# Hybrid decoder layer, float32: both MLP products as seven block products instead of eight, with the inner activations stored in HBM between them

## The reference, cut to what matters

```python
h = h + mix @ w_out                            # (520, 2048) @ (2048, 2048)
u = _rmsnorm(h, g_ffn)
h = h + jnp.square(jax.nn.relu(u @ w_up)) @ w_down   # w_up (2048, 8192), w_down (8192, 2048)
e = _rmsnorm(p_l @ w_ple, w_ple_norm) * jax.nn.sigmoid(h @ w_ple_gate)
y = _rmsnorm(h + e, g_final)
```

## Time and profile before

| | |
|---|---|
| median of 3 runs | 2850.12 us (2849.66 to 2850.43) |
| span of the profiled execution | 2847.1 us |
| output projection ends, MLP begins | about 1136 us into the span |
| MLP ends | about 2606 us |
| PE, DVE, ACT, POOL busy over the span | 95%, 46%, 27%, 20% |

### The profile page before, as it was taken

How to read it: one execution, slowest core, us unless ns; L and a number is a source line. 1 busy time by engine, 2 the same in 40 slices (tenths; PEclk the granted TensorE clock), 3 DMA queues, 4 the chain that set the end, 5 groups by cost and what they waited for, 6 DMA issues and landing times.

```text
span 2847.1 us, 50247 instructions
## 1 busy us (share of the span) xinstructions
PE 2696.2 (95%) x21759; PEld 2573.3 (90%) x21759; DVE 1320.5 (46%) x1501; ACT 774.8 (27%) x967; POOL 582.7 (20%) x290
## 2 busy tenths in 40 slices
PE   7999999967767999999999999999999999999998
PEld 7999999923346999999999999999999999999998
DVE  4277877628468224333333433333333333346433
ACT  3111111137643223222222222222222222223222
POOL 0098999300036011100000000000000000002322
PEclk9999999988876999999999999999999999999999
DMA  4388888489813222332333233333333333322233
GB/s 132 107 277 269 279 299 285 138 344 353 311 55 121 86 76 81 104 100 94 97 103 98 90 104 97 98 96 104 102 99 97 96 98 98 103 90 89 90 97 112
DMA packets 294896, 396.43 MB, mean 139 GB/s; under 512 B 14773, under 2 KB 256051, under 8 KB 292982
## 3 DMA queue, kind: packets, MB, share of 16 engines
q1 hardware_dynamic: 271688, 380.23, 40.4%
q10 hardware_dynamic: 22990, 13.01, 1.6%
HBM read 377.71 MB, written 15.58 MB: 138 GB/s over the span
## 4 chain that ended last, share of the span: by engine, by line
PE 79%; DVE 6%; POOL 5%; DMA 4%; issue 2%; SPq 2%; ACT 2%; ACTq 0%; DVEq 0%; POOLq 0%
PE ps L1180 25%; PE ps L1182 25%; PE ps L1185 25%; POOL kpage L1029 4%; DMA kpage<-in_cache_k 2%; DMA vpage<-in_cache_v 2%; DVE wl L1672 1%; PE ps L1280 1%; PE ps L1560 1%; SPq L470 1%; POOL dl L1074 1%; DMA xs<-in_x_sample 0%; ACT wh L608 0%; DVE se L1829 0%; POOL bx L1082 0%
## 5 line engine op out<-in xcount | busy, mean ns | idle before, releaser
L1180 PE MATMUL ps<-uh,wh 128*128 128x260 f32 x4512 | 1184.9, 284 | 20.1 <-DVE wl L1672 14.1
L1182 PE MATMUL ps<-ul,wh 128*128 128x260 f32 x4512 | 1180.5, 283 | 0.0
L1672 DVE TENSOR_TENSOR wl<-raw,wh 128x1024 fp32r<-128x1024 f32 (+1 forms) x418 | 590.4, 1413 | 1242.9 <-ACT wh L608 1242.8
L608 ACT ACTIVATE wh<-raw 128x1024 fp32r<-128x1024 f32 (+1 forms) x418 | 440.6, 1055 | 1803.6 <-PE ps L1185 1755.3
L1185 PE MATMUL ps<-uh,wl 128*128 128x260 f32 x4512 | 907.6, 283 | 0.0
L1180 PEld LDWEIGHTS ps<-uh,wh 128*128 128x128 f32 x4512 | 853.1, 189 | 22.9 <-DVE wl L1672 11.8
L1182 PEld LDWEIGHTS ps<-ul,wh 128*128 128x128 f32 x4512 | 851.3, 189 | 0.0
L1185 PEld LDWEIGHTS ps<-uh,wl 128*128 128x128 f32 x4512 | 696.4, 189 | 0.0
L1180 PE MATMUL ps<-hh,wh 128*128 128x260 f32 x2048 | 536.1, 283 | 0.0
L1182 PE MATMUL ps<-hl,wh 128*128 128x260 f32 x2048 | 534.1, 282 | 0.0
L1185 PE MATMUL ps<-hh,wl 128*128 128x260 f32 x2048 | 410.7, 282 | 0.0
(11 more groups left out here) (340 smaller groups left out, 1502.6 us busy)
## 6 DMA issues: line engine op xcount, KB each, us to landing
kpage<-in_cache_k SPq DMA_DIRECT2D x128, 512.0 KB, 4.9
vpage<-in_cache_v SPq DMA_DIRECT2D x128, 512.0 KB, 6.1
raw<-in_w_up SPq DMA_DIRECT2D x128, 512.0 KB, 3.6
raw<-in_w_down SPq DMA_DIRECT2D x128, 512.0 KB, 3.4
raw<-in_w_in SPq DMA_DIRECT2D x88, 512.0 KB, 4.6
raw<-in_w_out SPq DMA_DIRECT2D x32, 512.0 KB, 3.5
raw<-in_w_ple_gate SPq DMA_DIRECT2D x32, 512.0 KB, 3.4
xt<-in_x_prompt SPq DMA_DIRECT2D x8, 1024.0 KB, 9.0
```

What stands on the lines that cost most here:

```text
L608: A(wh[:, c % 2, 0:elems], raw[:, c % 2, 0:elems], ACT.Copy).then_inc(hi_ready, 1)
L1180: mm(ps[:, bank + 2 * m + f, 0:HALF], h_, xh[:, f * HALF:(f + 1) * HALF], start=st, stop=False)
L1182: mm(ps[:, bank + 2 * m + f, 0:HALF], h_, xl[:, f * HALF:(f + 1) * HALF], start=False, stop=False)
L1672: tt(wl[:, c % 2, 0:elems], raw[:, c % 2, 0:elems], wh[:, c % 2, 0:elems].bitcast(F32), ALU.subtract).then_inc(lo_ready, 1)
```

## The change

**Seven products.** A group of 256 weight columns is seen as 2 x 2 blocks: rows in even and odd tiles of 128, columns in two tiles of 128. The activations are seen as 2 x 2 blocks too: even and odd feature tiles, and two token halves. The 2 x 2 block product is made with seven block products of sums of blocks (Winograd's form) in place of eight. Products accumulate on PSUM banks (`BK`, `OPENS`): a bank's earlier product is read out by ACT or DVE, and a later product is then added on top of it.

**Units.** The work item is now a *unit*: 4 row tiles x 1 column tile x 1 token half x 3 = 12 matmuls, with 128 x 512 weight elements. ACT makes the high part (`unit_hi`), DVE the low part (`unit_lo`), in a ring of four. `w_up` takes 32 groups of 14 units, `w_down` 64 steps of 7 units: 896 units, 10,752 matmuls.

**Sums of weights.** Four of the seven products need sums of weight blocks. POOL makes them: `weight_sum`, 4 per group of `w_up`, 1024 elements each; `down_sum`, 4 per step of `w_down`, 512 elements each.

**Sums of activations.** For `w_up`, POOL makes them once (`operand_sum`), ACT and DVE split all seven operands into high and low parts. For `w_down`, each group of `w_up` gives 256 hidden features: ACT copies products out of PSUM, DVE adds (`hidden_add`, two of 520 elements) and applies relu and scale (`hidden_relu`, 1040 elements), ACT squares, POOL makes three sums (`hidden_sums`: 520, 260, 260 elements), ACT and DVE split (`hidden_hi`, `hidden_lo`).

**Through HBM.** The split hidden operands (7 x 520 numbers a partition, 1.86 MB a group) are stored to `hid_scr`, and come back in 8 parts of 7 loads (1.06 MB a load). All of `w_up` comes before all of `w_down`. The residual `h` goes through HBM too, since its place holds the operands of `w_up`. Each step of `w_down` adds its PSUM results to `hT` in six operations (`down_add`: four of 260 elements, two of 520).

**The weight rows** of `w_up` now come as 1 MB (two DMAs of 512 KB) into three buffers; `rows_used` lets buffer `m` go when its last `unit_lo` and its last `weight_sum` are done. The state updates move from the whole MLP to the `w_down` half. Many semaphores are shared in place of own ones. The core of the diff, blank lines left out:

```diff
-CHUNKS = D_FF // 512
+UPS = D_FF // 256
+PARTS = 8
+DOWNS = PARTS * (D_MODEL // 256)
+X_UP = 14 * UPS
+X_ALL = X_UP + 7 * DOWNS
...
+        hid_scr = nc.dram_tensor("hid_scr", (PARTS, 7, P, 4, T), F32, kind="Internal").ap()
...
+        BK = (3, 1, 0, 3, 2, 1, 3)
+        OPENS = (0, 1, 2, 4)
...
+            def rows_used(m):
+                g = m // 2
+                sp.wait_ge(q_lo, 14 * g + (10 if m % 2 else 2))
+                sp.wait_ge(s_sum, 4 * g + (3 if m % 2 else 4))
...
+            def store_hidden(g):
+                sp.wait_ge(o_hi, O_ALL + 4 * (g + 1))
+                sp.wait_ge(o_lo, O_ALL + 4 * (g + 1))
+                sp.dma_start(hid_scr[g // 4, :, :, g % 4, :].rearrange("i p x -> p i x"),
+                             hst.bitcast(F32).rearrange("p i s x -> p i (s x)")).then_inc(h_st, 16)
...
+            for g in range(UPS):
+                for m in (2 * g + 3, 2 * g + 4):
+                    if m < 2 * UPS and m >= 3:
+                        rows_used(m - 3)
+                        for hf in range(2):
+                            load_rows(m, hf)
+                if 1 <= g < UPS - 1:
+                    store_hidden(g - 1)
...
+            def unit_hi(x):
+                if x < X_UP:
+                    g, i = x // 14, x % 14 // 2
+                    if i in (0, 2, 4):
+                        m = 2 * g + (1 if i else 0)
+                        act.wait_ge(r_in[m % 3], 32 * (m // 3 + 1))
+                    else:
+                        act.wait_ge(s_sum, 4 * g + (1, 3, 5, 6).index(i) + 1)
+                else:
+                    n, i = (x - X_UP) // 7, (x - X_UP) % 7
+                    if i in (0, 2, 4):
+                        act.wait_ge(r_in[n % 2], down_landed(n) + 32)
+                    else:
+                        act.wait_ge(s_sum, 4 * UPS + 4 * n + (1, 3, 5, 6).index(i) + 1)
+                if x < 4:
+                    act.wait_ge(w_used, SL_PLE + x // 2 + 1)
+                else:
+                    act.wait_ge(q_used, x - 3)
...
+            def hidden_hi(g, k):
+                if k == 0:
+                    if g:
+                        act.wait_ge(h_st, 16 * 8 + 16 * g)
+                    act.wait_ge(x_q, g + 1)
+                    A(hst[:, 0:3:2, 0, :], tm[:, :, 0:HALF], ACT.Copy).then_inc(o_hi, 1)
+                    A(hst[:, 5, 0, :], tm[:, 1, HALF:T], ACT.Copy).then_inc(o_hi, 1)
+                elif k == 1:
+                    act.wait_ge(t_h, 3 * g + 2)
+                    A(hst[:, 1:4:2, 0, :], tb[:, 0:2], ACT.Copy).then_inc(o_hi, 1)
+                else:
+                    act.wait_ge(t_h, 3 * g + 3)
+                    A(hst[:, 4:7:2, 0, :], tb[:, 2:4], ACT.Copy).then_inc(o_hi, 1)
...
+            def weight_sum(g, k):
+                r1, r2 = rbuf[2 * g % 3], rbuf[(2 * g + 1) % 3]
+                a11, a21, a12, a22 = r1[:, :, 0:P], r1[:, :, P:2 * P], r2[:, :, 0:P], r2[:, :, P:2 * P]
+                n = 4 * g + k
+                if k == 0:
+                    for m in (2 * g, 2 * g + 1):
+                        pool.wait_ge(r_in[m % 3], 32 * (m // 3 + 1))
+                if n >= 3:
+                    pool.wait_ge(q_lo, 14 * g + (-6, -2, 0, 4)[k])
+                if k:
+                    pool.wait_ge(s_sum, n)
+                out = sring[n % 3]
+                s1, s2 = sring[4 * g % 3], sring[(4 * g + 1) % 3]
+                in0, in1 = ((a21, a22), (s1, a11), (a12, s2), (a11, a21))[k]
+                pool.tensor_tensor(out, in0, in1, ALU.subtract if k else ALU.add).then_inc(s_sum, 1)
...
+            def down_sum(n, k):
+                w = wbuf[n % 2]
+                a11, a21, a12, a22 = w[:, 0, :, 0:P], w[:, 0, :, P:2 * P], w[:, 1, :, 0:P], w[:, 1, :, P:2 * P]
+                if k == 0:
+                    pool.wait_ge(r_in[n % 2], down_landed(n) + 32)
+                if n == 0:
+                    pool.wait_ge(q_lo, X_UP - (2, 2, 0, 0)[k])
+                else:
+                    pool.wait_ge(q_lo, X_UP + 7 * (n - 1) + (2, 4, 6, 7)[k])
+                if k:
+                    pool.wait_ge(s_sum, 4 * UPS + 4 * n + k)
+                in0, in1 = ((a21, a22), (dring[0], a11), (a12, dring[1]), (a11, a21))[k]
+                pool.tensor_tensor(dring[k], in0, in1, ALU.subtract if k else ALU.add).then_inc(s_sum, 1)
...
+            def hidden_sums(g):
+                pool.wait_ge(x_q, g + 1)
+                if g:
+                    pool.wait_ge(o_hi, O_ALL + 4 * g)
+                    pool.wait_ge(o_lo, O_ALL + 4 * g)
+                pool.tensor_tensor(tb[:, 0:4:3], tm[:, :, HALF:T], halves(tm[:, 0]), ALU.subtract).then_inc(t_h, 1)
+                pool.wait_ge(t_h, 3 * g + 1)
+                pool.tensor_tensor(tb[:, 1], tm[:, 1, HALF:T], tb[:, 0], ALU.subtract).then_inc(t_h, 1)
+                pool.wait_ge(t_h, 3 * g + 2)
+                pool.tensor_tensor(tb[:, 2], tm[:, 1, 0:HALF], tb[:, 1], ALU.subtract).then_inc(t_h, 1)
...
+            for g in range(UPS):
+                if g + 1 < UPS:
+                    weight_sum(g + 1, 0)
+                if g:
+                    hidden_sums(g - 1)
+                if g + 1 < UPS:
+                    for k in range(1, 4):
+                        weight_sum(g + 1, k)
+            for n in range(DOWNS):
+                for k in range(4):
+                    down_sum(n, k)
+                if n == 0:
+                    hidden_sums(UPS - 1)
+                if n % 8 == 4:
+                    state_update(n // 8)
...
+            def unit(x, bank, opens, pairs, first, last):
+                pe.wait_ge(q_lo, x + 1)
+                out = ps[:, bank, 0:HALF]
+                for k in range(4):
+                    h_, l_ = whq[:, x % 4, k, :], wlq[:, x % 4, k, :]
+                    mm(out, h_, pairs[:, k, 0, :], start=(opens and first and k == 0), stop=False,
+                       skip_group_check=True)
+                    mm(out, h_, pairs[:, k, 1, :], start=False, stop=False, skip_group_check=True)
+                    z = mm(out, l_, pairs[:, k, 0, :], start=False, stop=(last and k == 3), skip_group_check=True)
+                z.then_inc(q_used, 1)
...
+            def unit_lo(x):
+                dve.wait_ge(q_hi, x + 1)
+                tt(wlq[:, x % 4], unit_weights(x), whq[:, x % 4].bitcast(F32), ALU.subtract).then_inc(q_lo, 1)
...
+            def hidden_lo(g, k):
+                src, at_ = ((tm[:, :, 0:HALF], slice(0, 3, 2)), (tb[:, 0:2], slice(1, 4, 2)),
+                            (tb[:, 2:4], slice(4, 7, 2)))[k]
+                dve.wait_ge(o_hi, O_ALL + 4 * g + (2, 3, 4)[k])
+                tt(hst[:, at_, 1, :], src, hst[:, at_, 0, :].bitcast(F32), ALU.subtract).then_inc(o_lo, 1)
+                if k == 0:
+                    tt(hst[:, 5, 1, :], tm[:, 1, HALF:T], hst[:, 5, 0, :].bitcast(F32), ALU.subtract)\
+                        .then_inc(o_lo, 1)
...
+            def down_add(n, k):
+                j, b = n % 8, down_bank(n)
+                dve.wait_ge(q_used, X_UP + 7 * n + (1, 2, 4, 5, 6, 7)[k])
+                if n in (0, 1, 3) and k == 0:
+                    dve.wait_ge(h_r[min(n, 2)], 16)
+                if n or k:
+                    dve.wait_ge(h_add, 6 * n + k)
+                c1, c2 = hT[:, 2 * j], hT[:, 2 * j + 1]
+                if k in (0, 1, 2, 3):
+                    c_ = (c1[:, 0:HALF], c2[:, HALF:T], c1[:, HALF:T], c2[:, 0:HALF])[k]
+                    ins = tt(c_, c_, ps[:, b + (3, 1, 3, 2)[k], 0:HALF], ALU.add)
+                elif k == 4:
+                    ins = tt(halves(c1), halves(c1), ps[:, b:b + 2, 0:HALF], ALU.add)
+                else:
+                    ins = tt(halves(c2), halves(c2),
+                             ps[:, b + 3, 0:HALF].unsqueeze(1).to_broadcast([P, 2, HALF]), ALU.add)
+                ins.then_inc(h_add, 1)
...
+            def beside(x):
+                if x < X_UP + 14:
+                    g, a = x // 14, x % 14
+                    if g and a in (1, 4):
+                        hidden_add(g - 1, a // 4)
+                    if g and a == 5:
+                        hidden_relu(g - 1)
+                    if g and a in (9, 10, 11):
+                        hidden_lo(g - 1, a - 9)
+                if x >= X_UP:
+                    n, i = (x - X_UP) // 7, (x - X_UP) % 7
+                    if i in (4, 5):
+                        down_add(n, i - 4)
+                    elif n and i < 4:
+                        down_add(n - 1, i + 2)
+                        down_add(n - 1, i + 2)
```

More of the change, by code:

```diff
@@ new lines, in _ @@
+            sp.wait_ge(h_st, 16 * 8)
+            sp.dma_start(uf[:, 0:3, :], h_scr[:, 0:3, :]).then_inc(h_r[0], 16)
+            rows_used(2 * UPS - 3)
+            load_down(1)
+            rows_used(2 * UPS - 2)
+            sp.dma_start(uf[:, 3:7, :], h_scr[:, 3:7, :]).then_inc(h_r[1], 16)
+            rows_used(2 * UPS - 1)
+            load_down(0)
+            store_hidden(UPS - 2)
+            for i in range(7):
```

(56 more changed lines are left out.)

651 lines of the change are left out of this document (385 added, 266 removed).

## The result

The changed kernel takes 2956.91 us (median of 4 runs, 2953.13 to 2962.45), the kernel before 2849.89 beside it: ratio 1.038, 95% interval 1.0365 to 1.0395. It is slower, 35 us more than the 2922 forecast and inside the range. The profiled execution has a span of 2960.7 us, 113.6 more than before. (In the diff above, the last line of DVE's `beside` stands twice by a slip; the kernel has it once.)

A forecast was written before the change was run, and what follows sets the result against it. PE paced the old MLP; after the change, shared DVE/POOL turns and a chain bound `w_up`. +62 - 32 + 20 + 20 + 2 = +72 on 2847.1, span 2919, plus 3.0 around it: 2922 us, range 2785 to 3040.

The forecast's parts named there:

- The turns: DVE operations with two SBUF inputs and POOL operations alternate by whole instruction: 23.7 us a `w_up` group, 9.3 a `w_down` step.
- The chain: `w_up`: fourth sum, rows' load, first sum, hidden sums, ACT's high parts, PE's unit 10; 25.0 us a group, +62.
- the bound of 23.7: `w_up`: lower bound in us for a group, DVE's and POOL's shared turns added up, against PE's 20.1.
- that rival: PE's clock falls to 0.83 in `w_up`: some 26.5 us a group, 2970 us in all; chance 0.07.
- -32: `w_down`: 64 steps at 11.0 us in place of 11.5, a gain of 32 us.
- about 0.9 is not: `w_down` step: of the six DVE adds, about 0.9 us is not hidden in POOL turns, 9.3 becoming 10.2.
- Some 0.4 for handing over: `w_down` step: 0.4 us added for handing over, on the way from 10.2 to 11.0 us.
- the port sum of 9.3: `w_down` step: DVE low parts 4.2 us plus POOL sums 5.1, taking turns, against PE's 10.06.
- 0.4 a step: `w_down`: cost of state updates, 6.2 us every 8 steps or 0.8 a step, partly in PE's slack.
- The first rival: `w_down` at PE's 10.06 us a step, `w_up` at 23.7 a group: 2810 us, or 2790; chance 0.20.
- +40: Start of the MLP +20 us (8 to 32) and changeover between the halves +20 (8 to 35).
- the wait for the parts: Changeover: a hidden store and three parts pass before PE goes past `w_down` unit 0, four more follow; in the +20.

The follow-up runs named there:

- the fills: Against the changed kernel, each of POOL's weight sums became two constant fills that read nothing, so products use constants: 2777.86 us, ratio 0.9756.
- taking one link out: Against the changed kernel, POOL's hidden sums were queued ahead of the next group's first weight sum: 2905.29 us, ratio 1.020.
- the half-change: Changed kernel with plain `w_up`, seven products in `w_down` alone, state updates in `w_up`, late reload, four parts issued earlier: 2791.17 us, ratio 0.9798.

## Why the prediction was right, and where its sizes were off

**The mechanism held.** The turns between two-input DVE operations and POOL were read from three places of the trace before; the fills confirm them with POOL still busy. That the result is inside the range says little, for the range of 255 us reached from faster to slower; what supports the mechanism is the rows and the runs.

**`w_up`: right, some 0.9 us too small.** The chain went through the instructions named, and taking one link out brought the group to 24.1, beside the bound of 23.7. The term that was mis-sized is the chain, 25.9 in place of 25.0. Part may be the clock: it was 0.93 to 0.96, not the 0.83 of that rival, and its share is left open.

**`w_down`: right sign, -48 in place of -32.** The step that failed is "about 0.9 is not" (hidden) and "Some 0.4 for handing over": ordinary steps run at 10.1, so the port sum of 9.3 with its extras fits under PE. What lifts the mean is above all the state updates, 4.5 us each, where 0.4 a step (3.2 each) was taken; their operations take 7.3 us beside DVE, not 6.2. The first rival's condition (a step under some 10.3) was met in 30 of the 48 steps from 8 to 55, but not by their mean; `w_up`, the start and the changeover ran against that rival in full.

**Start and changeover: +63 in place of +40.** The work was named, most of the waits were not. At the start it is the third rows' buffer, which lies over the operands' sources, and so is loaded last. At the changeover the wait for the parts was named and is 15 us; what was not named is the load of the fourth step's weights behind SyncE's wait, 10 us of PE's time.

The misses are +32, -16, +10, +13, and nothing at the end: +39 on the forecast's span, of 41.6 in all. That the total is only 35 us off is in part luck: without the gain of 16 in `w_down` it would have been some 2973 us, outside the forecast's own range of 2880 to 2970. And what lies around the span is 1.8 us in the profiled execution (2962.45 in all), not the 3.0 that the forecast added.

## What to carry to other kernels

When a change moves work to POOL, add up POOL's reading operations and DVE's two-SBUF-input operations as if they ran on one engine, and compare that sum with PE's time for the same stage: here 23.7 against 20.1 in one stage and 9.3 against 10.06 in the other told which half would gain, and the half-change gained 2.0%. Spreading operations over steps of the same stage gave 4 us here; moving them to a stage where the shared way is idle was part of the kernel that gained. In a queue in order, put what others wait for ahead of the instruction that waits for HBM: one exchange of two calls was worth 52 us here. And what a new stage reads first has to be issued well before the old one ends: the parts, issued 4 us ahead, cost 15 us.

## What the runs showed of the hardware

- A POOL fill beside DVE's two-input operations holds neither up: 128 fills of 1024 elements take 0.942 to 0.962 us, and DVE's low parts stay at 0.69. A POOL sum of the same size takes 2.5 to 2.8 us and makes DVE's 0.69 into 0.96 to 1.59.
- DVE's busy time includes its waits for POOL: from 1400 to 1600 us, 176 operations show as 191 us with the hidden sums first, and 198 operations as 133 us with the fills.
- The granted clock (a mean between its levels of 1.2 and 2.4 GHz) fell to 0.81 at the start of the MLP, where PE was busy 39 of 64 us, and stood at 0.96 where it was busy 170 of 200, but at 1.00 where it was busy 171 of 200 in even groups of 24.1 us.
- Loads of 1040 KB from HBM, seven issued in a row, landed 2.5 us apart, and from 2000 to 2005 us, with every engine still, the DMAs of this one core moved 426 GB/s. The prediction had 350 from the key pages and quotes 358.
